# Two weight chunks of each small expert multiplied as fp32 products, without the split into high and low parts

## What is computed

```
def expert_block(args):
    tok, e = args
    xb = hf[tok]
    gu = xb @ w_gate_up[e] + b_gate_up[e]          # 1024 x 2048
    gate, up = jnp.split(gu, 2, axis=-1)
    gate = jnp.minimum(gate, SWIGLU_LIMIT)
    up = jnp.clip(up, -SWIGLU_LIMIT, SWIGLU_LIMIT)
    act = (up + 1.0) * gate * jax.nn.sigmoid(SWIGLU_ALPHA * gate)
    return act @ w_down[e] + b_down[e]             # 1024 x 1024
```

## Time and profile before

| | |
|---|---|
| median of 3 runs | 1766.94 us (1766.47 to 1767.54) |
| the profiled execution | 1766.66 us, of which the span of the profile is 1764.9 us |
| PE busy | 1698.8 us (96%) |
| DVE busy | 1381.7 us (78%) |
| ACT busy | 1200.8 us (68%) |
| POOL busy | 713.1 us (40%) |
| granted TensorE clock | 0.998 of full speed on average |
| the pairs of experts | from about 700 us to 1690 us of the span, 65.8 us each |

### The profile page before, as it was taken

One profiled execution on the slowest core, in us unless ns is written; L12 is line 12 of the kernel. 1 busy time (PEld: TensorE's weight loads), 2 busy tenths in 40 slices (PEclk: granted clock), 3 DMA queues, 4 the chain that ended last, 5 costly groups with the idle time before them and its releaser, 6 DMA issues.

```text
span 1764.9 us, 24895 instructions
## 1 busy us (share of the span) xinstructions
PE 1698.8 (96%) x8477; PEld 1346.8 (76%) x8477; DVE 1381.7 (78%) x1048; ACT 1200.8 (68%) x967; POOL 713.1 (40%) x344
## 2 busy tenths in 40 slices
PE   6999999999999999999999999999999999999998
PEld 5878889777888987767767767767767767767776
DVE  4666776755334389999999999999999999999984
ACT  5565555433223368788788788788788788788775
POOL 6124233550000072355465365365365365365110
PEclk9999999999999999999999999999999999999999
DMA  5443343433336469999999999999999999999951
GB/s 177 122 129 85 121 122 107 121 108 119 96 96 231 164 218 397 391 404 392 399 402 392 399 401 392 402 406 388 404 404 391 405 400 398 402 400 395 408 201 49
DMA packets 150865, 504.64 MB, mean 286 GB/s; under 512 B 12733, under 2 KB 73285, under 8 KB 117173
## 3 DMA queue, kind: packets, MB, share of 16 engines
q1 hardware_dynamic: 141652, 478.49, 70.0%
q0 software_dynamic: 9104, 25.28, 6.0%
q10 hardware_dynamic: 48, 0.07, 0.0%
HBM read 487.63 MB, written 20.28 MB: 288 GB/s over the span
## 4 chain that ended last, share of the span: by engine, by line
PE 68%; DVE 14%; issue 9%; ACT 6%; POOL 2%; DVEq 0%; ACTq 0%; POOLq 0%
PE gu_ps L2395 13%; DVE split_l L1928 9%; PE gu_ps L2147 8%; PE gu_ps L2149 8%; PE gu_ps L2148 8%; PE dn_ps L2453 7%; PE gu_ps L2399 7%; PE dn_ps L2459 3%; ACT split_h L1303 3%; PE gu_ps L2409 2%; PE dn_ps L2652 1%; PE gu_ps L2652 1%; PE et_ps L2381 1%; DVE up_sb L1915 1%; PE gu_ps L2169 1%
## 5 line engine op out<-in xcount | busy, mean ns | idle before, releaser
L1928 DVE TENSOR_TENSOR split_l<-ring,split_h 128x2048 fp32r<-128x2048 f32 x384 | 864.8, 2285 | 71.0 <-ACT split_h L1303 69.3
L1303 ACT ACTIVATE split_h<-ring 128x2048 fp32r<-128x2048 f32 x384 | 729.9, 1913 | 113.8 <-PE gu_ps L2399 62.7
L914 POOL COPY icur<-slots 96x1 int32 x30 | 282.8, 9428 | 412.3 <-PE et_ps L2381 410.1
L1536 DVE TENSOR_TENSOR w_lo<-w_raw,w_hi 128x2048 fp32r<-128x2048 f32 (+1 forms) x45 | 104.3, 2318 | 128.8 <-ACT w_hi L1035 122.6
L2409 PE MATMUL gu_ps<-split_l,xgT_h 128*128 128x512 f32 x480 | 139.6, 412 | 17.8 <-DVE split_l L1928 14.0
L2147 PE MATMUL gu_ps<-hT_h,w_hi 128*128 128x512 f32 x392 | 154.6, 394 | 0.6 <-DVE acc L1589 0.6
L2149 PE MATMUL gu_ps<-hT_h,w_lo 128*128 128x512 f32 x392 | 152.7, 390 | 0.0
L2148 PE MATMUL gu_ps<-hT_l,w_hi 128*128 128x512 f32 x392 | 152.6, 389 | 0.0
L2395 PE MATMUL gu_ps<-split_h,xgT_h 128*128 128x512 f32 x512 | 140.6, 396 | 0.9 <-DVE xgT_l L1934 0.9
L2399 PE MATMUL gu_ps<-split_l,xgT_h 128*128 128x512 f32 x512 | 137.2, 390 | 0.0
L2395 PE MATMUL gu_ps<-split_h,xgT_l 128*128 128x512 f32 x512 | 137.2, 390 | 0.0
(11 more groups left out here) (426 smaller groups left out, 3242.1 us busy)
## 6 DMA issues: line engine op xcount, KB each, us to landing
ring<-in_w_gate_up SPq DMA_DIRECT2D x256, 1024.0 KB, 8.0
ring<-in_w_down SPq DMA_DIRECT2D x128, 1024.0 KB, 9.2
w_raw<-in_w_in SPq DMA_DIRECT2D x28, 1024.0 KB, 5.9
arow<-acum_rows POOLq DMA_DIRECT2D x16, 512.0 KB, 6.5
w_raw<-in_w_ssd_out SPq DMA_DIRECT2D x8, 1024.0 KB, 5.4
w_raw<-in_w_in SPq DMA_DIRECT2D x9, 512.0 KB, 6.1
w_raw<-in_w_mix_out SPq DMA_DIRECT2D x4, 1024.0 KB, 7.9
wpg<-in_w_ple_gate SPq DMA_DIRECT2D x2, 2048.0 KB, 19.9
```

Source lines behind the costliest of these rows:

```text
L914: g.tensor_copy(icur[:, :], col).then_inc(idx_done, 1)
L1303: a.activation(split_h[s % SPLIT][:, :], ring[s % RING][:, :], ACT.Copy).then_inc(hi_done, 1)
L1536: v.tensor_tensor(w_lo[RAW_SLOT[n]][:, 0:size], w_raw[RAW_SLOT[n]][:, 0:size], w_hi[HI_SLOT[n]][:, 0:size].bitcast(F32), ALU.subtract).the ...
L1928: v.tensor_tensor(split_l[s % SPLIT][:, :], ring[s % RING][:, :], split_h[s % SPLIT][:, :].bitcast(F32), ALU.subtract).then_inc(lo_done, 1)
```

## The change

The fifth gate-up chunk (`WHOLE_UP`, s-up 4) and the third down chunk (`WHOLE_DN`, s-down 2) of every small expert are no longer split. PE waits for their load itself and multiplies the raw weights in the ring by the same stationary tile, read as fp32: 4 fp32 matmuls of 512 columns (`whole_gate_up`, `whole_down`) in place of 8 fp32r ones. ACT's `high` and DVE's `low` of these chunks go; the chunk before them counts for two in `hi_done` and `lo_done`. Since such a chunk used no split buffer, the high part of the chunk three after it waits for an older one (`back=2 * SPLIT`). Its ring slot is free only when PE has used it, so the two loads that follow into these slots wait for `chunk_used` in place of `lo_done` (`after_whole`). SP's loop over experts becomes one over pairs, with the same DMAs. The new core of the diff:

```diff
             def gate_up(j, e, i, of, k, first=False, after_whole=False):
                 slot = (UP + i) % RING
-                if not first:
+                if after_whole:
+                    sp.wait_ge(chunk_used, chunk_at(j, e, i) - RING + CHUNKS + 1)
+                elif not first:
                     sp.wait_ge(lo_done, chunk_at(j, e, i) + 1)
...
-            def high(j, e, i):
+            def high(j, e, i, parts=1, back=SPLIT):
                 at, s = chunk_at(j, e, i), UP + i
                 act.wait_ge(e_loaded[s % RING], raw_loaded(j, e, i))
-                act.wait_ge(chunk_used, at + CHUNKS - SPLIT + 1)
-                a.activation(split_h[s % SPLIT][:, :], ring[s % RING][:, :], ACT.Copy).then_inc(hi_done, 1)
+                act.wait_ge(chunk_used, at + CHUNKS - back + 1)
+                a.activation(split_h[s % SPLIT][:, :], ring[s % RING][:, :], ACT.Copy).then_inc(hi_done, parts)
...
+            def raw_weights(e, i):
+                slot = (UP + i) % RING
+                pe.wait_ge(e_loaded[slot], raw_loaded(0, e, i))
+                alone(pe)
+                return ring[slot]
+
+            def whole_gate_up(e, i, k):
+                raw = raw_weights(e, i)
+                for b in range(4):
+                    o = t.matmul(gu_ps[:, b * 512:b * 512 + 512], xgT_h[:, k, :].bitcast(F32),
+                                 raw[:, b * 512:b * 512 + 512], start=False, stop=False)
+                o.then_inc(chunk_used, 1)
...
-                    if half:
+                    if half and r == WHOLE_DN:
+                        whole_down(e, r)
+                    elif half:
                         half_down(e, r)
...
                 for k in range(2, UP):
-                    half_gate_up(e, k, k)
+                    if k == WHOLE_UP:
+                        whole_gate_up(e, k, k)
+                    else:
+                        half_gate_up(e, k, k)
```

More of the change, by code:

```diff
@@ L1387, in one_pass, with rest @@
                     high(j, 0, i)
-                def rest(e, more, rows_in, rows_act, folds=None):
+                def rest(e, more, rows_in, rows_act, folds=None, whole_up=False, whole_down=False):
                     turned_high(t0 + 3 + e * 2, xgT_h, rows_in, 1.0 if more else 1.0 / ALPHA)
                     for i in range(12, 14):
-                        high(j, e, i)
+                        high(j, e, i, 1, 2 * SPLIT if folds is not None and i == CHUNKS + 1 else SPLIT)
                     if folds is not None:
@@ L1419, in half_expert @@
                     high(j, e, 11)
[L1420 removed]
+                    rest(e, True, ROWS, HALF, whole_down=True)
                 if isinstance(j, int):
@@ L1922, in up, with low @@
                                        ).then_inc(act_done, 1)
-            def low(j, e, i):
+            def low(j, e, i, parts=1):
                 at, s = chunk_at(j, e, i), UP + i
@@ L1978, in one_pass, with rest @@
                     low(j, 0, i)
-                def rest(e, more, rows_act):
-                    for i in range(12, 16):
+                def rest(e, more, rows_act, whole_up=False, whole_down=False):
+                    for i in range(12, 15):
                         low(j, e, i)
+                    low(j, e, 15, 2 if whole_up else 1)
                     if more:
@@ L1986, in rest, with expert @@
                         turned_low(t0 + 4 + e * 2, dst, actT_h, rows_act, 1.0 / ALPHA)
-                        for i in range(16, 22):
+                        if not whole_up:
+                            low(j, e, 16)
+                        for i in range(17, 21):
                             low(j, e, i)
-                def expert(e, more, half_next=False):
+                        low(j, e, 21, 2 if whole_down else 1)
+                def expert(e, more, half_next=False, whole_down=False):
                     up(ROWS, chunk_used, chunk_at(j, e, UP - 1) + CHUNKS + 1, n0 + e + 1)
-                    low(j, e, 10)
+                    if not whole_down:
+                        low(j, e, 10)
                     low(j, e, 11)
@@ L1998, in expert @@
                         turned_low(t0 + 3 + e * 2, xgT_l[:, :, 0:ROWS], xgT_h, ROWS, 1.0 if more else 1.0 / ALPHA)
-                    rest(e, more, ROWS)
+                    rest(e, more, ROWS, half_next)
                 def half_expert(e, folds):
```

53 lines of the change are left out of this document (37 added, 16 removed).

## The result

The changed kernel takes 1780.24 us (median, 1775.75 to 1785.15) beside 1766.86 (1766.35 to 1767.54) for the kernel before; the ratio is 1.0076, with an interval of 1.0064 to 1.0088. Measured again beside the experiments it was 1.0071 (1.0058 to 1.0084). The forecast was 1760.7, faster, with a range of 1754 to 1769; the time lies outside, on the side of rival 2.

A forecast was written before the change was run, and what follows sets the result against it. Bound: the engines' own loop, 65.8 us a pair, with DMA close behind at about 65.4. From 1766.66: -5 DMA idle time, -1.8 lead, +0.5 last whole s-down 2, +0.3 to the median, giving 1760.7 us; range 1754 to 1769.

The forecast's parts named there:

- rival 2: Pairs: late loads of s-up 4 let the DMA run dry, up to 1.4 us a pair, +20, 1786 us; chance 0.14.
- What bounds the kernel: Expert pairs: engines' own loop 65.8 us and DMA about 65.4; PE bounds the large stretch, DVE the small.
- The room: DMA idle time in the pairs, all the loads let the kernel gain: about 6 us in all, 5 taken.
- What goes: Per pair two low parts of 2.25 us on DVE and two high parts of 1.90 us on ACT.
- What comes: Per pair twice four fp32 matmuls for eight fp32r: 3.43 us a chunk, 1.62 more on PE, 3.24 a pair.
- The small stretch: PE takes over from DVE; ends at some 28.5 us, not 29.6; engines' loop 1.1 to 1.4 us shorter a pair.
- What takes it back, the lead: Loads can't follow; engines run ahead of them once, at most some 1.8 us, bounded by l-down 2's landing.
- The added waits: s-up 4's load issued 1.4 us later, l-down 2's at about 1166 instead of 1164.8; both expected to cost nothing.
- the reserve: Queue ahead of s-up 4's load lasted 1.9 us longer than needed, so its 1.4 us delay fits in.
- Rival 1: No change: the idle share is an artefact, the floor stands at the present time, only the lead remains, 1765.5; chance 0.25.

The follow-up runs named there:

- small transfers: Gathers and scatters cut to 16 rows in place of 96 or 48: kernel before 0.9998, 65.79 us a pair; changed kernel 0.9944, 65.10.
- 5.2 us of PE's work left out: Changed kernel with early slot release, late gather and only one of four fp32 products per whole chunk: 0.9992, 65.60 us a pair.
- the run on the kernel before: Kernel before, only SP's wait changed: s-up 4's load waits until PE has used s-down 2; 1.0002, 65.78 us a pair.
- the gather is held: Changed kernel, small stretch's row gather waits until PE has used s-up 2: 0.9986 and 0.9996, pairs of 65.62 and 65.68 us.
- ACT's copy first: Changed kernel, ACT does its copy for the join ahead of l-down 1's high part: 1.0085, 66.79 us a pair.

## Why the prediction was wrong, step by step

- **What bounds the kernel.** Right: an engines' loop of 65.8 us (shown with small transfers: 65.79) and a DMA floor just below. The floor was mis-sized: I put it at 65.4 from DMA shares of 1.00 to 1.02, and it is 65.60 (measured with 5.2 us of PE's work left out). Those shares can't tell it: the changed kernel reads 1.01 at 393 GB/s, before 1.01 at 399. The room was 0.2 us a pair, some 3 us in all, and not 5.
- **What goes.** Right, 30 high and 30 low parts.
- **What comes.** Right for the chunk: 3.46 and 3.43 us in the chain above, from the end of the matmul before it, where 3.43 was forecast.
- **The small stretch.** The mechanism was right (PE takes over from DVE), the size half: 28.95 us in place of the 28.5 walked through, and 65.10 a pair is 0.7 less than before, not 1.1 to 1.4. The split small chunks cost PE 1.81 us in a row of s-down chunks, but 1.83 to 1.98 in s-up, and I had used 1.81 for all.
- **What takes it back, the lead.** This failed. I bounded the engines' lead over the loads by l-down 2 and found 1.8 us. The tightest landing is that of l-down 1: its high part waited for the load already in the kernel before (it starts 0.1 us after the landing in nearly every pair), and in the changed kernel those of s-up 5 to l-down 0 do so too. There was no lead to spend.
- **The added waits.** This is the step that failed and decided: I put their cost at nothing, and together with the earlier gather it is 1.1 us a pair. The delay itself was right: measured from PE's first matmul of s-down 0, s-up 4's load is issued after 8.1 us (1282.19 to 1290.28) where it was 6.5 (1143.17 to 1149.65), so 1.6 us later, 1.4 forecast (my 1151.0 should read 1150.9). Of this load I said that it isn't late, and alone it doesn't cost anything (1.0002). But the reserve was counted with the gather behind these loads, and what I didn't follow is GpSimd. Taking the low part of s-down 2 from DVE was costed as a gain for DVE only, while GpSimd's copy had stood behind DVE's row of low parts for 10 us, and that had kept the gather behind the loads of s-up 4 to l-down 0. It came some 10 us earlier, into just the stretch from which the late release had taken the reserve. Neither alone costs over 0.3%, both together 0.76%.
- **The rivals.** Rival 2 named the sign (chance 0.14) and a size of up to 20 us, pairs over 66 and landings of s-up 4 near 4.8 us after issue; 13.4 us, 66.9, and 5.0 to 7.4 came. The idle DMA engines that it names are there too (0.92). But its mechanism was the release alone, and the run on the kernel before has them as well (0.91) at no cost. That the sign was met is thus half luck. Rival 1 (no change) is what the change gives once the gather is held.

## What to carry to other kernels

When work is taken off an engine, list what else that engine's work has held back, on the other queues too: a transfer that comes earlier is not free if the loads are close to their limit. A DMA share near 1 is no measure of the room that is left. The GB/s in windows of a few us show where the rate is lost, and the floor is measured by taking the engines' work away and then the bytes. And where a landing is waited for in every pass, follow the loop from landing to release to issue to landing; if it is the longest, cutting any one path through it can leave a twin, as ACT's order did.

## What the hardware showed unexpectedly

A copy of 96 indices on GpSimd takes 1.05 us in one place and 10.34 in another, and both end 0.04 to 0.05 us behind the end of one of DVE's low parts; what decides behind which one isn't shown. When the copy began before the row of low parts and took 0.18 us (ACT's copy first, large stretch), the gather instruction behind it took 13.4 us instead: GpSimd was held either way.

```profile
1254.35 0.18 POOL L929 COPY icur<-slots 96x1 int32 x1 [20.09 <-PE et_ps L2407]
1255.40 13.38 POOL L920 DMA_INDIRECT xg<-h_rows,icur  x1 [0.88 <-POOL icur L929]
```

The DMA engines read busy 1.02 of a window while they move 359 GB/s, where the loads alone reach 430.
